# Order of the last output half, of the expert rows' transposes and of one weight slot's loads in a decoder layer step

## The reference, cut to what matters

```python
xp = xp + mix_out(a_out, b_out, w_out[l])        # output projection, 1024 x 1024, and residual
xp = xp + moe(rmsnorm(xp, ln2_g[l]))             # the same for xs, the 8 sample rows

def hier_moe(h, w_rg, b_rg, w_re, b_re, w_gate, w_up, w_down):
    pg = softmax(h @ w_rg + b_rg); gi = argmax(pg)            # best of 4 groups
    le_sel = (h @ w_re + b_re) of that group                  # 8 experts in it
    top_p, top_i = top_k(softmax(le_sel), 2)                  # two of them, gates normalised
    ...
    a, b = einsum('nd,edf->nef', h, w_gate), einsum('nd,edf->nef', h, w_up)
    hid = silu(a) * b * gates
    return einsum('nef,efd->nd', hid, w_down)                 # 32 experts, 1024 -> 128 -> 1024
```

## Time and profile before

| | us |
|---|---|
| median of 3 runs | 441.01 (438.19 to 441.26) |
| span of the profiled execution | 437.3 |
| TensorE busy | 397.0 (91% of the span) |
| VectorE busy | 214.6 (49%) |
| ScalarE busy | 150.9 (34%) |
| GpSimd busy | 70.5 (16%) |

### The profile page before, as it was taken

The page is one execution under the profiler, slowest core; times in us unless marked ns, Lnnn a source line. Parts: engine busy times, 40 slices in busy tenths (PEclk is TensorE's granted clock), DMA queues, the critical chain, the costliest instruction groups (busy, mean ns, idle before and its releaser), DMA issues. The chain is left out here.

```text
span 437.3 us, 6404 instructions
## 1 busy us (share of the span) xinstructions
PE 397.0 (91%) x2466; PEld 211.0 (48%) x2466; DVE 214.6 (49%) x442; ACT 150.9 (34%) x321; POOL 70.5 (16%) x59
## 2 busy tenths in 40 slices
PE   1999998999799999999989998979999999999782
PEld 1454443443244434455533557756555555554551
DVE  2968345799597465455351525741222312222276
ACT  5724122132364455454332435211222312222043
POOL 0000113444350100000000000220323223211000
PEclk9999999899899999999999999788999999999897
DMA  8981530874935133940069994899999999994384
GB/s 290 357 245 49 194 96 0 305 273 135 328 117 194 42 101 124 302 157 1 6 222 411 411 414 174 257 375 396 338 409 414 410 410 407 403 402 169 125 332 192
DMA packets 42323, 109.17 MB, mean 250 GB/s; under 512 B 7864, under 2 KB 8632, under 8 KB 42288
## 3 DMA queue, kind: packets, MB, share of 16 engines
q1 hardware_dynamic: 36000, 94.79, 58.8%
q0 software_dynamic: 5856, 12.81, 7.8%
q10 hardware_dynamic: 432, 1.11, 0.8%
HBM read 100.00 MB, written 16.94 MB: 267 GB/s over the span
## 5 line engine op out<-in xcount | busy, mean ns | idle before, releaser
L1540 PE MATMUL bank<-weights_split,tokens_split 128*128 128x512 f16 (+1 forms) x648 | 151.2, 387 | 2.1 <-DVE x L1260 1.4
L1540 PEld LDWEIGHTS bank<-weights_split,tokens_split 128*128 128x128 f16 (+1 forms) x648 | 61.8, 98 | 81.1 <-issue 12.7
L636 POOL TENSOR_TENSOR big<-big,middle 128x1536 f32<-128x1536 f32 x8 | 27.8, 3469 | 93.9 <-DMA middle<-sample_q 52.3
L1848 PE MATMUL bank<-big,tokens_split 128*64 128x256 f32 x320 | 39.0, 399 | 1.6 <-ACT tokens_split L945 1.6
L1438 DVE TENSOR_TENSOR middle<-bank,middle 128x128 f32<-128x128 f32 x16 | 4.7, 293 | 59.2 <-ACT middle L950 59.2
L1848 PEld LDWEIGHTS bank<-big,tokens_split 128*64 128x64 f32 x320 | 23.9, 143 | 13.7 <-ACT tokens_split L945 2.1
L1019 DVE SCALAR_TENSOR_TENSOR weights_split<-middle,weights_split 128x1024 f16<-128x1024 f32 x16 | 20.8, 1333 | 12.8 <-ACT weights_split L738 12.7
L1797 PE MATMUL bank<-half_consts 128*128 128x256 f16 x186 | 23.8, 294 | 2.9 <-issue 2.9
L1515 PE MATMUL bank<-ident,big 128*128 128x128 f32 (+1 forms) x92 | 14.6, 295 | 12.7 <-DVE big L1029 9.3
L670 POOL DMA_INDIRECT tokens_split<-h_rows,middle x16 | 16.3, 1018 | 59.1 <-PE bank L1837 46.0
L822 ACT ACTIVATE middle<-bank 128x128 f32<-128x128 f32 (+3 forms) x32 | 13.9, 435 | 32.0 <-PE bank L1588 31.8
(11 more groups left out here) (199 smaller groups left out, 542.8 us busy)
## 6 DMA issues: line engine op xcount, KB each, us to landing
big<-in_w_gate SPq DMA_DIRECT2D x10, 1024.0 KB, 13.8
big<-in_w_up SPq DMA_DIRECT2D x10, 1024.0 KB, 17.5
big<-in_w_down SPq DMA_DIRECT2D x10, 1024.0 KB, 15.2
middle<-in_w_in SPq DMA_DIRECT2D x16, 512.0 KB, 6.6
big<-in_cache_win_k SPq DMA_DIRECT2D x24, 256.0 KB, 3.9
middle<-in_cache_win_v SPq DMA_DIRECT2D x24, 256.0 KB, 4.6
big<-in_w_out SPq DMA_DIRECT2D x8, 512.0 KB, 8.4
big<-expert_rows SPq DMA_DIRECT2D x8, 512.0 KB, 6.9
```

Of the source, the lines that this page charges most:

```text
L636: nc.gpsimd.tensor_tensor(prod[:, :, :], kring[:, b % 2], qb[:, b % 2, :].unsqueeze(1).to_broadcast([P, NPAT, W]), ALU.mult).then_inc(prod ...
L1540: ins = T.matmul(out, (hT if rows is None else rows)[:, high_low, k if rows is None else k - 4, tokens], wg[:, place, part, k, columns], s ...
L1848: ins = T.matmul((ptb, ovb)[b][e * CAP:(e + 1) * CAP, 0:2 * FE], xT[:, b, k, e * CAP:(e + 1) * CAP], places[slot][:, 0:2, e, k * FE:(k + 1 ...
```

## The change

Three edits come together. First, in the second output half the sample rows are finished fourth and tile 3 last; all counts that went by tile number go by position. Second, in the expert loop pairs 1 and 2 are transposed as before, and from then on the rows of pair j+2 at the end of pair j. Third, the loads of slot 6 stand right behind the stores of x, ahead of those of slot 5, with waits for the stores, the transposes, the products and the squares that read x; down of slot 2 and gate of slot 4 go out before the store of tile 3.

```diff
+EARLY_ROWS = 2
-for _h in range(2):
-    UNITS += [("out", 2 * t + _h) for t in range(3)] + [("part", _h)]
-    UNITS += [("out", 2 * t + _h) for t in range(3, NT)]
+OUT_ORDER = [0, 1, 2, NT - 1, 3]
+UNITS += [("out", 2 * t) for t in range(3)] + [("part", 0)] + [("out", 2 * t) for t in range(3, NT)]
+UNITS += [("out", 2 * t + 1) for t in range(3)] + [("part", 1)] + [("out", 2 * t + 1) for t in OUT_ORDER[3:]]
...
-TURNS += [("h2", 2 * t + c) for t in range(NT) for c in range(2)]
+TURNS += [("h2", 2 * t + c) for t in OUT_ORDER for c in range(2)]
...
@@ sync @@
             gate_up_load(sp, 4, 1)
             down_load(sp, 4)
-            for t in range(NT):
+            def store_x(t):
                 left(sp, ("out", 2 * t + 1))
                 sp.dma_start(dram_rows(x2_dram, t), x[0:rows_of(t), t, :]).then_inc(x_stored, 16)
-            sp.wait_ge(acc_ready, UNIT[("out", 2 * NT - 1)] + 1)
+
+            for t in OUT_ORDER[:NT - 1]:
+                store_x(t)
+            sp.wait_ge(acc_ready, len(UNITS))
             down_load(sp, 2)
             gate_up_load(sp, 4, 0)
-
+            store_x(OUT_ORDER[NT - 1])
+
+            sp.wait_ge(x_stored, 16 * NT)
+            sp.wait_ge(tp_ready, len(TURNS))
+            sp.wait_ge(times_gain, 2 * NT)
+            sp.wait_ge(sq2, 2 * NT)
+            gate_up_load(sp, 6, 0)
+            gate_up_load(sp, 6, 1)
+            down_load(sp, 6)
             for t in range(NT):
                 sp.wait_ge(h2w[t], 16)
             sp.wait_ge(r_done, NT)
...
             gate_up_load(sp, 5, 0)
-            sp.wait_ge(x_stored, 16 * NT)
-            gate_up_load(sp, 6, 0)
-            gate_up_load(sp, 6, 1)
-            down_load(sp, 6)
@@ gpsimd @@
-            for t in range(NT):
-                pool.wait_ge(h2_ready, t + 1)
-                pool.dma_start(h2_dram[t * P:t * P + rows_of(t), :], h2n[0:rows_of(t), t % 2, :]).then_inc(h2w[t], 16)
+            for at, t in enumerate(OUT_ORDER):
+                pool.wait_ge(h2_ready, at + 1)
+                pool.dma_start(h2_dram[t * P:t * P + rows_of(t), :], h2n[0:rows_of(t), at % 2, :]).then_inc(h2w[t], 16)
@@ scalar @@
+            square2(NT - 1, 1)
+            root2(NT - 1)
+            scale_h2(NT - 1)
+            turn_x2(NT - 1, 0)
+            turn_x2(NT - 1, 1)
             square2(3, 1)
+            root2(3)
             turn_x2(3, 0)
             turn_x2(3, 1)
-            root2(3)
             scale_h2(3)
-            turn_x2(NT - 1, 0)
-            square2(NT - 1, 1)
-            turn_x2(NT - 1, 1)
-            root2(NT - 1)
-            scale_h2(NT - 1)
...
                     silu(base + j, j % 2)
-                    if j + 1 < PAIRS:
+                    if j < EARLY_ROWS:
                         copy_x(base + (j + 1), (j + 1) % 2)
...
                     copy_hidden(base + j, j % 2)
+                    if EARLY_ROWS <= j + 1 < PAIRS - 1:
+                        copy_x(base + (j + 2), j % 2)
@@ vector @@
             def times(t, half):
-                n = rows_of(t)
-                if half == 0 and t >= 2:
-                    dve.wait_ge(h2w[t - 2], 16)
+                n, at = rows_of(t), OUT_ORDER.index(t)
+                if half == 0 and at >= 2:
+                    dve.wait_ge(h2w[OUT_ORDER[at - 2]], 16)
...
-            for t in range(NT - 1):
+            for t in range(3):
                 add_out(t, 1)
...
                 times(t, 0)
                 times(t, 1)
-                if t >= 2:
-                    logits(t - 2)
+            logits(0)
+            inverse(2)
+            add_out(NT - 1, 1)
             times(NT - 1, 0)
+            times(NT - 1, 1)
+            logits(1)
+            inverse(NT - 1)
+            add_out(3, 1)
+            times(3, 0)
+            times(3, 1)
+            logits(2)
             inverse(3)
-            logits(2)
-            add_out(NT - 1, 1)
-            times(NT - 1, 1)
-            inverse(NT - 1)
-            logits(NT - 2)
             logits(NT - 1)
+            logits(3)
@@ tensor @@
             def router(t, half):
...
-                    pe.wait_ge(logits_done, t - 1)
+                    pe.wait_ge(logits_done, at - 1)
...
             quarters(1, 6)
-            project_out(3, 1)
+            x_turns(2, 0)
+            x_turns(2, 1)
             router(1, 0)
             router(1, 1)
-            x_turns(2, 0)
-            x_turns(2, 1)
             quarters_sum(1, ("out", 2 * NT - 1))
+            project_out(3, 1)
+            x_turns(NT - 1, 0)
+            x_turns(NT - 1, 1)
             router(2, 0)
             router(2, 1)
             x_turns(3, 0)
             x_turns(3, 1)
-            x_turns(NT - 1, 0)
-            router(3, 0)
-            x_turns(NT - 1, 1)
-            router(3, 1)
             router(NT - 1, 0)
             router(NT - 1, 1)
+            router(3, 0)
+            router(3, 1)
...
-            def turn_x(n, b):
+            def turn_x(n, b, first=False):
 
                 pe.wait_ge(x_landed[b], gathered(n, b))
+                if not first:
+                    pe.wait_ge(xt_a, n)
+                    pe.wait_ge(xt_d, n)
...
-                turn_x(base, 0)
+                turn_x(base, 0, isinstance(base, int))
                 for j in range(PAIRS):
                     gate_up(base, j)
-                    if j + 1 < PAIRS:
+                    if j < EARLY_ROWS:
                         turn_x(base + (j + 1), (j + 1) % 2)
                     if j >= 1:
                         down(base, j - 1)
...
                     turn_hidden(base + j, j % 2)
+                    if EARLY_ROWS <= j + 1 < PAIRS - 1:
+                        turn_x(base + (j + 2), j % 2)
                 down(base, PAIRS - 1)
```

More of the change, by code:

```diff
@@ L880, in square2 @@
                 total = stat[0:n, 64 + t:65 + t] if half == 0 else stat[0:n, 16 + t:17 + t]
-                if t > 0:
-                    act.wait_ge(sq2, NT * half + t)
+                at = OUT_ORDER.index(t) if half == 1 else t
+                if at > 0:
+                    act.wait_ge(sq2, NT * half + at)
                 nc.scalar.activation(sbk[half][0:n, :], x[0:n, t, cols_], ACT.Square, scale=D ** -0.5,
@@ L906, in scale_h2 @@
             def scale_h2(t):
-                n = rows_of(t)
-                act.wait_ge(rms_inverse, t + 1)
-                act.wait_ge(times_gain, 2 * t + 2)
-                rows = h2n[0:n, t % 2, :]
+                n, at = rows_of(t), OUT_ORDER.index(t)
+                act.wait_ge(rms_inverse, at + 1)
+                act.wait_ge(times_gain, 2 * at + 2)
+                rows = h2n[0:n, at % 2, :]
                 nc.scalar.activation(rows, rows, ACT.Copy, scale=stat[0:n, 16 + t:17 + t]).then_inc(h2_ready, 1)
@@ L1276, in inverse @@
                 v = stat[0:rows_of(t), 16 + t:17 + t]
-                dve.wait_ge(rooted, NT + t + 1)
+                dve.wait_ge(rooted, NT + OUT_ORDER.index(t) + 1)
                 V.reciprocal(v, v).then_inc(rms_inverse, 1)
             def logits(t):
-                n = rows_of(t)
-                dve.wait_ge(r_done, t + 1)
-                dve.wait_ge(rms_inverse, t + 1)
-                V.scalar_tensor_tensor(out=L[0:n, t, :], in0=(ptb, ovb)[t % 2][0:n, 0:36],
+                n, at = rows_of(t), OUT_ORDER.index(t)
+                dve.wait_ge(r_done, at + 1)
+                dve.wait_ge(rms_inverse, at + 1)
+                V.scalar_tensor_tensor(out=L[0:n, t, :], in0=(ptb, ovb)[at % 2][0:n, 0:36],
                                        scalar=stat[0:n, 16 + t:17 + t], in1=rbias[0:n, :],
@@ L1718, in router @@
             def router(t, half):
[L1719 removed]
+                n, at = rows_of(t), OUT_ORDER.index(t)
                 src = x_rowsT[t % 2] if t < NT - 1 else x_sampleT
                 wait_turned_out(pe, ("h2", 2 * t + half))
[L1722 removed]
+                if at == 0:
                     pe.wait_ge(fin_copied, 1)
[L1724 removed]
+                elif at == 1:
                     pe.wait_ge(att_low, NT - 1)
                 else:
[L1727 removed]
+                    pe.wait_ge(logits_done, at - 1)
                 for k in range(4 * half, 4 * half + 4):
[L1729 removed]
+                    ins = T.matmul((ptb, ovb)[at % 2][0:n, 0:36], src[:, k, 0:n], wr[:, k, :],
                                    start=k == 0, stop=k == KD - 1)
@@ L1801, in _ @@
             pe.wait_ge(picks, 1)
-            left(pe, ("out", 2 * NT - 1))
+            left(pe, UNITS[-1])
             picked = [O[:, k * NT:(k + 1) * NT, :] for k in range(2)]
```

18 lines of the change are left out of this document (8 added, 10 removed).

## The result

The changed kernel takes 441.5 us (median of 20 runs, 437.7 to 444.6) against 437.3 us for the kernel before beside it: a ratio of 1.0093, 95% interval 1.0066 to 1.012. So it is about 0.9% slower. The profiled execution took 443.4 us; its span, 441.4 us, answers to the 437.3 of the earlier trace rows, 4.1 us more. The time is 2.0 us above the span in this execution as in the others, not the 3.7 that the forecast took from a median of three runs.

The account below looks back on a forecast made before the run. TensorE's gapless chain of sixteen 6.75 us pairs was taken as the bound, so only its start could move the end. Terms −3.0 + 2.5 + 0.3 − 0.5 = −0.7 gave span 436.6, plus 3.7: 440.3 us, range 436.0 to 444.2.

Parts of the forecast that it names:

- what bounds the kernel: Expert stage: sixteen pairs of 6.75 us fill TensorE without a gap, so only the chain's start can move the end.
- no pair waits for weights now: Expert loop: weight loads hold up no pair, so slot 6's earlier loads gain nothing on TensorE.
- Reordering inside it takes nothing off: Expert loop: a pair is 6.75 us of TensorE whatever its order; transposes two pairs ahead cost zero in the steady loop.
- The sum: Whole span: −3.0 + 2.5 + 0.3 − 0.5 = −0.7 us on 437.3, so 436.6.
- Gather: First gather of expert rows: falls into 5 MB of loads, lands in 6.9 us instead of 4.4; 2.5 us more.
- Routing: Second output half to last logits: sample rows fourth ends the logits at 273.1 instead of 276.10; 3.0 us less.
- clock rival: Clock falls in the reordered stretch or before the rank matmuls: 1.7 of the 3.0 us go, 443 us; chance 0.12.
- The short gap: Before the first pair, if the gather is unhurt: 2.4 GHz kept, first gate and up 2.3 us less, 435.5; within chance 0.27.
- Gathers did not set the pace: Rival, expert loop: gathers set the pace from a landing of 10.8 us; 446 us at 11.8; chance 0.07.
- the rows of pair 2: Start of expert loop: wanted at 308.55 instead of 312.15, 0.6 us late at the median landing; 0.3 us more taken.
- the last h2 store: Rival, before the first gather: now 0.5 MB, it could release the gather instead of the tables; 443.3 or 440.6; chance 0.07.
- Tail: Loop's end: with 3 MB of loads gone the last scatter is quick, so VectorE's last copy comes sooner; 0.5 us less.

Follow-up runs that it names:

- e11_after_upfirst: The changed kernel with gate and up weights of the last two pairs asked for ahead of their down weights; ratio to the kernel before 0.9985.
- e6_fewer_bytes: The kernel before with transposes two pairs ahead, and half the down weights of pairs 7 to 10 not loaded (2 MB less); ratio 0.9961.
- e8_up_first: The changed kernel with slot 6's loads as before, and the last two pairs' gate and up weights asked for ahead of their down weights; ratio 0.990.
- edits 1 and 3: Sample rows fourth (1) and transposes two pairs ahead (3), without slot 6's earlier loads (2); together 0.9991, alone 0.9971 and 1.0032.
- e13_no_slot6: The changed kernel with the loads as before (slot 6 late again), new row order and transposes two pairs ahead kept; ratio to the kernel before 0.9991.
- e7_ahead_old_place: The kernel before with transposes two pairs ahead, but at the old place right behind gate and up, gathers one pair earlier; 441.4 us, one run, no ratio.
- the four comparisons above: Kernels differing by the slot edit: 0.9991 becomes 1.0093; with the better order of last loads 0.990 becomes 0.9985; by itself 1.0096 and 1.0115.
- e5_slot5_late: The changed kernel with slot 5's up and down loads (2 MB) asked for behind the table and flag, not ahead of the first gather; ratio 1.0021.
- e12_slot6_only: The kernel before with only slot 6's three loads moved earlier, loads of slots 2 and 4 left behind all five row stores; ratio 1.0096.
- e1_order: The kernel before with the new order of rows alone (sample rows fourth in the second output half); ratio 0.9971.
- e10_short_tail: The changed kernel with 85 filler matmuls behind the expert stage in place of 100; 440.9 us, ratio to the kernel before 1.005.
- after: The changed kernel itself, all three edits together, against the kernel before; ratio 1.0093.
- e9_late5_upfirst: The changed kernel with slot 5's up and down loads behind the table, last two pairs' gate and up ahead of down, 85 fillers; ratio 0.9913.
- e3_ahead: The kernel before with the transposes two pairs ahead alone; ratio 1.0032.
- e2_slot6: The kernel before with the new place of slot 6's loads alone, two other loads ahead of the last row store; ratio 1.0115.

## Why the prediction was wrong

**The time came near by luck.** 441.5 us is 1.2 from the forecast's 440.3. But the forecast was a change of −0.7 us on 441.0, the median of three runs; over 20 runs the kernel before takes 437.3, and the change is +4.2.

**The step that failed** is the conclusion of the part on what bounds the kernel, that only the start of the chain of pairs can move the end, and with it the sentence "no pair waits for weights now", from which the late or early loads were costed at nothing. Both sides of the earlier trace rows were read, TensorE 50.00 of 50.00 us and DMA 0.98, and the second was passed over. No wait doesn't mean room: the last up weights landed 0.4 us ahead of use. From gate and up 13 on the changed kernel takes 3.72 us more than before, waits and low clock together, and in e11_after_upfirst this is gone; e6_fewer_bytes and e8_up_first take the limit away in kernels without the slot edit. The forecast had no rival for it. By its terms edits 1 and 3 without the slot edit were worth −3.0 + 0.3 = −2.7 us, a ratio of 0.994; e13_no_slot6 gave 0.9991 (0.9955 to 1.0028).

**"Reordering inside it takes nothing off"** was wrong too, by 0.30 us a pair and 3.32 us in all. The forecast took a pair for a sum of fixed durations; e7_ahead_old_place shows that the order sets them. The two errors all but cancel, which is why the pairs' total changed by only 0.62 us.

**The sum.** For that reason the miss stands in other rows of the table: of the 4.8 us between −0.7 and the +4.1 of the two spans, routing and tail make 1.4 each, the gather 1.2, the way from the logits to the table 0.4 and the pairs 0.3. The slot edit as a whole was forecast at +2.5 − 0.5 = +2.0 us; by the four comparisons above it costs 0.85 to 1.15%, 3.7 to 5.0 us.

**Gather: right mechanism, mis-sized.** The mechanism, a first gather among slot 6's and slot 5's loads, is shown by e5_slot5_late and e12_slot6_only. The landing took 7.8 us, not the 6.9 borrowed from the third gather, and the term was +3.4 instead of +2.5, inside its bounds of 0 and 4.5. The forecast also laid the whole delay to slot 6; in e8_up_first, without the slot edit, the earlier table alone brought the gather near enough to slot 5's loads for 6.6 us. The Trainium skill, "DMA: Bandwidth & Descriptors", section "Queues, rings and completion order", says that an increment lands only after every earlier write of its engine. The landings agree better with this than with the same section's taking of turns, from which the forecast worked out an estimate of 5.7 us: with slots 6 and 5 ahead the gather took 6.1 to 8.7 us, and with slot 5's 2 MB alone it was the quicker the longer ago they were asked for (3.4 us ago 6.6 in e8_up_first, 4.4 ago 4.4 before, 6.2 ago 3.8 in e1_order), as if it waited for them.

**Routing: right at one clock level.** 257.4 to 273.1 was forecast, 15.7 us from the quarters to the logits. Where the clock held (e13_no_slot6, e8_up_first, e10_short_tail) it took 15.46 to 15.58 us; where it fell (after, e1_order, e5_slot5_late, e9_late5_upfirst, e11_after_upfirst) 17.70 to 17.84. The forecast set the new order at the high level against the old one at the low level. At the low level on both sides the gain is 0.8 us (18.63 to 17.79), at the high level 1.8 (17.29 in e7_ahead_old_place, where the clock held to 271.5, to 15.5). The forecast's clock rival came true in the profiled execution; it left 1.3 us of the gain, the trace 0.8. The low level was priced at 1.7 us, though by the forecast's own rows sixteen router matmuls alone lose 2.0 (3.7 instead of 1.70); the runs show 2.3 (17.8 against 15.5). The reason given for the high level, a stretch without a gap over half a microsecond, did not hold: in the changed kernel TensorE has no gap above 0.17 us between 257 and 269 us, and the clock fell.

**Rivals.** The short gap that lets the first gate and up keep 2.4 GHz is real: in the runs, gaps of 1.05 to 1.39 us left it at 3.67 us, those of 2.75 and more put it at 5.20 to 6.62, and between them both occurred (5.92 at 1.95, 3.67 at 2.00 and 2.25). Gathers did not set the pace (no wait for rows after the third pair); the rows of pair 2 arrived in time here, and in e3_ahead 0.64 us late, as the forecast worked out for the median landing; and the last h2 store did not take the place of the table, with whose instruction (L1404) the gather's wait ends.

**Tail.** +0.91 us instead of −0.5. The term itself came out: the last copy on VectorE starts 0.04 us behind the last down (407.79), not 0.54, and no longer waits for a scatter. But the gap of 2.54 us inside the fillers, which the forecast did not have, outweighs it: the mixing follows the fillers at once, where before it waited 0.62 and 1.28 us for rows. Every kernel here that transposes two pairs ahead, e7_ahead_old_place too, has such a gap; before, e1_order, e2_slot6 and e12_slot6_only run the fillers as one block.

## What to carry to other kernels

A busy share of 1.00 on one engine doesn't settle what binds: where the DMA share is 0.98 beside it, look up when the last transfer landed and when it was used, for that slack (0.4 us here) caps what an earlier or shorter chain can gain unless the loads come sooner too. A load asked for sooner may only move a hole in the transfers: here they stood still from 300 to 302 us for want of a free slot. On its way it may delay a small transfer on the critical path. Where loads set the end, order the last ones by when they are first used.

## What the runs showed of the hardware

- The same fp32 matmuls and transposes take 6.75 us or 6.45 us a pair by their order alone; fewer changes between 64-column and 128-column weights go with the shorter time.
- The same code on the same stretch of routing is granted 2.4 GHz in one execution and 1.2 in another (15.58 us in e10_short_tail, 17.79 in the changed kernel), with TensorE busy and no gap above 0.17 us in the 12 us ahead of the fall. What decides it stays open.
- TensorE issued nothing for 1.8 to 2.5 us inside a block of 85 or 100 identical matmuls, after the first seven or eight, in every kernel that transposes two pairs ahead. What it waited for the profile doesn't show, and no run here separates it. A transfer of an instruction queue lies near the start of the gap (at 411.8 in the changed kernel, with the gap from 411.7), but the kernel before has one too, at 408.0, and no gap.
